# The output projection of a hybrid encoder layer as seven block products of half size, with its weight sums made during the convolution's output units

## The chip, the cores and the metric

The kernel runs on one core of one Trainium2 chip. The metric is the device time of one execution in microseconds (us), taken several times; the median counts. Beside the times there is one profiled execution, from which all durations below come. The core's engines run side by side, each with a queue of its own that it takes in order: TensorE multiplies matrices (the profile calls it PE, and PEld its weight loads), VectorE (DVE) and GpSimd (POOL) work on tiles element by element, ScalarE (ACT) applies functions and copies, SyncE (SP) issues DMAs. ScalarE issues DMAs too. They wait for one another by semaphores.

## What is computed

One layer of an encoder over 768 tokens of width 1024 (512 of a prompt, 256 of a sample, and 16 learned tokens ahead of each request). The part around the change, cut from the reference:

```python
c = jax.nn.silu(_layernorm(c, conv_ln_g[l], conv_ln_b[l]))
conv = c @ w_conv_out[l]                               # 1024 x 1024
g_a, g_c = jnp.split(jax.nn.sigmoid(gate_logits + b_gate[l]), 2, axis=-1)
h = h + (g_a * attn + g_c * conv) @ w_out[l]           # 1024 x 1024: the output projection
u = _rms(h, norm_mlp[l])
h = h + jnp.square(jax.nn.relu(u @ w_mlp_in[l])) @ w_mlp_out[l]     # the mixer, hidden 4096
```

All of it is fp32.

## The kernel before

**Products.** An fp32 product is made of three products in a rounded format (fp32r): both operands are split into a high part (rounded) and a low part (what rounding left), and high x high, high x low and low x high are added up in PSUM. So for every weight there is a supply chain. A *unit* of weights is 128 x 1024 values. SyncE loads it into one of four slots of `raw` (line 479 and, for the output projection, line 558), ScalarE rounds it into one of two `whi` (`hi_unit`, 348 to 352), GpSimd (in the stages here; elsewhere VectorE) makes the low part in one of two `wlo` (`lo_unit`, 354 to 357), TensorE multiplies. `hi_unit` of unit n waits until TensorE is through with unit n - 2, since it overwrites that one's `whi` (semaphore `unit_used`). SyncE loads a unit when the low part of the unit three before it exists.

**Stages around the change**, in TensorE's order:

1. The attention's output (`w_o_attn`), 8 units.
2. The convolution's output (`w_conv_out`, lines 2122 to 2125): 8 units, each 48 matmuls of 384 columns that fill one 128-row block m of the result. Unit m waits until block m - 2 has been read out of PSUM (`merged`).
3. The output projection (`w_out`, `token_major`, lines 2127 to 2152): tokens stand on the partitions, two halves of 512 output columns, each 4 units x 36 matmuls of 512 columns, 288 in all; 6 token tiles, one PSUM bank each. In the last unit, tile by tile, each tile's last products are followed by its addition to h on VectorE (`h_add`), its root mean square and scaling, and, ahead of the last tile, by the first transposes of the normalised rows (`first_transposes`, line 2168).
4. The mixer's first product (`w_mlp_in`), whose pairs of hidden blocks are already computed with seven half-size products instead of eight (lines 2186 to 2218; sums of weights are made by `in_sum`, and blocks of u by sums of rows), and its second product in the same manner.

**The loop over the convolution's output blocks.** For block m VectorE (1431 to 1439) multiplies the unit's result by the gate (`gconv`), adds it to the attention's part (`zacc`, semaphore `merged`), waits for ScalarE's rounding of it and makes the low part `zlo`. ScalarE (912 to 916) rounds the weights of unit m + 1 of this stage and then block m of z:

```python
for m in range(KD):
    if m > 0:
        hi_unit(act, U_CO, m // 4, m % 4 + 1)
    act.wait_ge(merged, KD + m + 1)
    nc.scalar.activation(zhi[:, m], zacc[:, m], ACT.Copy).then_inc(z_hi, 1)
```

**During the projection.** The mixer's second product needs sums of blocks of its weight. ScalarE issues their loads (`load_sums`, line 946) and stores (`store_sums`), VectorE makes them (`weight_sums`, lines 1507 to 1518, four operations of 128 x 1024 for each of two at the projection's start), ScalarE squares the rows of h (`h_square`). At the end VectorE makes four `in_sum` between the first and the last `h_add` of the second half, the reciprocals (`h_recip`), the scaling (`h_scale`, some of it on GpSimd, lines 1831 to 1836) and the low parts of the transposed rows (`u2_lo`).

## Time and profile before

| what | value |
|---|---|
| median of 3 runs | 1246.15 us (1245.69 to 1247.12) |
| the profiled execution's own time | 1246.2 us |
| its span in the trace | 1244.1 us |
| TensorE busy | 1214.2 us, 98% of the span |
| TensorE's weight loads | 1097.8 us, 88% |
| VectorE busy | 930.8 us, 75% |
| ScalarE busy | 584.7 us, 47% |
| GpSimd busy | 184.6 us, 15% |

The shares are means over stages. A stage is read by itself: how much of it TensorE is busy, at which granted clock (PEclk, 1.00 is the full 2.4 GHz), and which engine's work ends last ahead of each of TensorE's waits. In a row, `out<-in` are the names of tiles, `L948` is line 948, `x4` the number of instructions that the row holds, and what stands in brackets is the idle time of the engine ahead of the instruction, with the work whose end ended it.

### The profile page before, as it was taken

Reading aid. Unit: us, or ns where it says so; the run is one execution under the profiler, and the core shown is the slowest. Engines: PE = TensorE matmul, PEld = TensorE weight load, DVE = VectorE, ACT = ScalarE, POOL = GpSimd, SP = SyncE. Lnnn points to the kernel's source line nnn. Section 1 sums busy time; section 2 is a strip of 40 time slices with the busy share of each in tenths; the row PEclk is TensorE's granted clock in tenths of the full one; section 3 lists DMA queues with packets and bytes.
Section 4 is the critical chain, followed back from the end, with each engine's and each line's share of the span. In section 5 each row is a group of like instructions: output and inputs, shape, how many; then the busy total and the mean of one; then the engine's idle time right before and its main releaser. Section 6 shows DMA issues by size and latency. Waiting matters only on the chain.

```text
span 1244.1 us, 17971 instructions
## 1 busy us (share of the span) xinstructions
PE 1214.2 (98%) x6833; PEld 1097.8 (88%) x6833; DVE 930.8 (75%) x1192; ACT 584.7 (47%) x933; POOL 184.6 (15%) x148
## 2 busy tenths in 40 slices
PE   7999999999999999999999998899999999999997
PEld 5888888888889999989999887899999988888886
DVE  4799999998857777776653527888777767688865
ACT  6211122632246766773531136666666664444452
POOL 2000000000025444436423333000000000000001
PEclk9999999999999999999999999999999999999999
DMA  7212222334220110205335643356888459633332
GB/s 210 68 51 67 65 63 68 93 119 118 82 74 17 33 31 13 68 1 149 108 105 215 262 132 131 108 179 234 279 272 272 164 176 352 198 121 135 129 125 102
DMA packets 144370, 161.40 MB, mean 130 GB/s; under 512 B 11197, under 2 KB 111611, under 8 KB 142122
## 3 DMA queue, kind: packets, MB, share of 16 engines
q1 hardware_dynamic: 132848, 114.13, 29.5%
q10 hardware_dynamic: 11450, 46.30, 10.1%
q8 instruction: 46, 0.75, 0.2%
q14 instruction: 26, 0.21, 0.1%
HBM read 124.76 MB, written 35.65 MB: 129 GB/s over the span
## 4 chain that ended last, share of the span: by engine, by line
PE 84%; DVE 5%; ACT 4%; issue 3%; POOL 2%; ACTq 0%; POOLq 0%; DVEq 0%
PE psum L424 36%; PE psum L2236 16%; PE psum L2215 16%; PE psum L2149 4%; PE psum L2013 4%; PE psum L2045 2%; PE psum L1884 1%; POOL lnacc L1814 1%; PE psum L2025 1%; PE psum L1971 1%; DVE acc L1208 1%; PE psum L1853 1%; POOL wlo L357 1%; DVE wlo L1502 1%; ACT whi L352 0%
## 5 line engine op out<-in xcount | busy, mean ns | idle before, releaser
L2215 PE MATMUL psum<-ub,whi 128*128 128x384 f32 x896 | 229.6, 337 | 7.6 <-ACT r L942 2.3
L1208 DVE SCALAR_TENSOR_TENSOR acc<-cs,convw,acc 128x799 f32<-128x799 f32 x232 | 230.2, 1056 | 0.2
L352 ACT ACTIVATE whi<-raw 128x1024 fp32r<-128x1024 f32 (+1 forms) x80 | 79.5, 994 | 280.0 <-PE psum L424 244.5
L2215 PEld LDWEIGHTS psum<-ub,whi 128*128 128x128 f32 x896 | 162.0, 189 | 10.3 <-issue 6.5
L424 PE MATMUL psum<-uhi,wlo 128*128 128x512 f32 x592 | 152.8, 339 | 0.0
L424 PE MATMUL psum<-uhi,whi 128*128 128x512 f32 x592 | 152.2, 338 | 0.5 <-DVE wlo L357 0.5
L424 PE MATMUL psum<-ulo,whi 128*128 128x512 f32 x592 | 152.6, 339 | 0.0
L357 POOL TENSOR_TENSOR wlo<-raw,whi 128x1024 fp32r<-128x1024 f32 (+2 forms) x37 | 83.2, 2249 | 462.7 <-ACT whi L352 462.7
L2215 PE MATMUL psum<-ub,wlo 128*128 128x384 f32 x448 | 150.4, 336 | 0.0
L424 PEld LDWEIGHTS psum<-uhi,whi 128*128 128x128 f32 x592 | 91.4, 188 | 13.9 <-issue 0.8
L424 PEld LDWEIGHTS psum<-uhi,wlo 128*128 128x128 f32 x592 | 91.7, 188 | 12.9
L424 PEld LDWEIGHTS psum<-ulo,whi 128*128 128x128 f32 x592 | 91.4, 188 | 12.3
L1055 ACT ACTIVATE hidhi<-hid 128x768 fp32r<-128x768 f32 x56 | 47.4, 846 | 107.6 <-PE psum L2236 106.0
L1599 DVE TENSOR_TENSOR hidlo<-hid,hidhi 128x768 fp32r<-128x768 f32 x56 | 53.6, 957 | 44.5 <-ACT hidhi L1055 44.5
L2215 PEld LDWEIGHTS psum<-ub,wlo 128*128 128x128 f32 x448 | 84.5, 189 | 0.0
L1844 POOL TENSOR_SCALAR h<-h,rstd 128x512 f32<-128x512 f32 x3 | 3.7, 1240 | 465.0 <-DVE rstd L1675 465.0
L357 DVE TENSOR_TENSOR wlo<-raw,whi 128x1024 fp32r<-128x1024 f32 (+1 forms) x39 | 47.0, 1206 | 26.1 <-ACT whi L352 26.1
L2236 PE MATMUL psum<-whi,hidhi 128*128 128x512 f32 x168 | 65.5, 390 | 0.1
L2236 PE MATMUL psum<-wlo,hidhi 128*128 128x512 f32 x168 | 65.4, 389 | 0.0
L2236 PE MATMUL psum<-whi,hidlo 128*128 128x512 f32 x168 | 65.4, 389 | 0.0
L2236 PE MATMUL psum<-fhi,hidlo 128*128 128x512 f32 x168 | 65.4, 389 | 0.0
L2236 PE MATMUL psum<-fhi,hidhi 128*128 128x512 f32 x168 | 65.4, 389 | 0.0
(264 smaller groups left out, 2663.7 us busy)
## 6 DMA issues: line engine op xcount, KB each, us to landing
raw<-in_w_in SPq DMA_DIRECT2D x38, 512.0 KB, 3.9
wst<-in_w_mlp_out ACTq DMA_DIRECT2D x16, 1024.0 KB, 7.1
wsum<-wst ACTq DMA_DIRECT2D x16, 1024.0 KB, 5.5
raw<-in_w_mlp_in SPq DMA_DIRECT2D x32, 512.0 KB, 4.7
raw<-wsum SPq DMA_DIRECT2D x32, 512.0 KB, 3.9
raw<-in_w_mlp_out SPq DMA_DIRECT2D x24, 512.0 KB, 4.8
gates<-gout ACTq DMA_DIRECT2D x16, 384.0 KB, 2.4
gin<-gates SPq DMA_DIRECT2D x16, 384.0 KB, 3.0
```

Of the source, the lines that this page charges most:

```text
L352: nc.scalar.activation(whi[:, c % 2, 0:w], raw[:, c % 4, 0:w], ACT.Copy).then_inc(hi_ready, 1)
L357: eng.tensor_tensor(out=wlo[:, c % 2, 0:w], in0=raw[:, c % 4, 0:w], in1=whi[:, c % 2, 0:w].bitcast(F32), op=ALU.subtract).then_inc(lo_read ...
L424: mm = nc.tensor.matmul(out[:, o0:o0 + n], a, b[:, k, c0:c0 + n], start=first and step == 0, stop=last and step == 2)
L1055: nc.scalar.activation(hidhi[u % 4][:, :, :], f_block(n, c), ACT.Copy).then_inc(hidhi_ready, 1)
L1208: ins = nc.vector.scalar_tensor_tensor(out=a, in0=src, scalar=w, in1=a, op0=ALU.mult, op1=ALU.add)
L1502: nc.vector.tensor_tensor(out=wl, in0=in_source(s, j), in1=wh.bitcast(F32), op=ALU.subtract).then_inc(lo_ready, 1)
L1599: nc.vector.tensor_tensor(out=hidlo[u % 4][:, :, :], in0=f_block(n, c), in1=hidhi[u % 4][:, :, :].bitcast(F32), op=ALU.subtract).then_inc( ...
L2013: mm = nc.tensor.matmul(psum[:, q % 2, e * HALF:e * HALF + n], a[:, c0:c0 + P], b[:, grp["k0"] + k0:grp["k0"] + k0 + n], start=step == 0, ...
L2045: mm = nc.tensor.matmul(bank[:, 7, 0:2 * P], a[:, vt, hh * VD:(hh + 1) * VD], r[:, blk % 2, e, :], start=e == 0 and step == 0, stop=False)
L2149: mm = nc.tensor.matmul(out, a, b[:, kk, :], start=first and step == 0, stop=last and step == 2)
L2215: mm = nc.tensor.matmul(bank[:, IN_BANK[s % 2][j], 0:TH], a[:, k], b[:, k], start=j in (0, 1, 2, 5) and k == 0 and step == 0, stop=k == 3 ...
L2236: mm = nc.tensor.matmul(bank[:, P_BANKS[n % 2][tt]], a, b[:, kk, :], start=c == 0 and kk == 0 and step == 0, stop=c == PU - 1 and kk == 1 ...
```

## The change

The output projection takes seven products of half size (half of the sum's length, half of the columns, half of the tokens) in place of eight: with A the two halves of tokens by the two halves of the sum, B the weights' quarters, four products use sums and differences of blocks of z and of w_out (`OUT_WEIGHT`: "t" marks a product on a sum of weights, "w" one on w_out itself). It now has 14 units of 18 matmuls of 512 columns, 252 in all. A product is added to one quarter of h or stands in PSUM until others are added to it there (`OUT_BANK`), and a quarter of h is filled by additions in a table's order (`OUT_ADD`, `OUT_ON`, `OUT_FREE`).

- The sums of w_out (`out_sums`, four operations of 128 x 1024 for each of two halves c) are made on VectorE in the loop over the convolution's output blocks, in the passes m = 0 and 1, between two steps of z. ScalarE issues their loads of 4 x 1 MB ahead of that loop, behind the wait for the last low part of c, and their stores to DRAM in the passes m = 1 and 2. SyncE loads them back as units.
- In that loop ScalarE rounds, for m < 4, two 384-wide pieces of z in place of one of 768: the second after VectorE has made a difference; for m >= 4 one of 768. VectorE makes differences and low parts (two or three more operations of 384 per block). Three further blocks of z, 128 x 1536 each, are rounded and made low in the projection itself (`z_block_hi`, `z_block_lo`).
- The mixer's `weight_sums` 0 and 1 no longer stand ahead of the first `h_add` but in pieces between the `h_add` of the products. Both `load_sums` are issued ahead of the rounding of the projection's unit 1.
- The first transposes stand between units 12 and 13 of the projection: the first token rows are complete after the sixth product. In `in_sum`'s place among the last `h_add`, two now follow the scaling of tile 2 and two that of tile 5. GpSimd scales tile 0 ahead of its last `lo_unit`.
- Slots, counts of semaphores and the numbers of units are shifted to fit (`raw` slots by two, since 14 units and not 8 go before the mixer; the first weight buffer `wst` to another address); two semaphores of the layer norm become one.

The core of the diff:

```diff
@@ tables
+OUT_WEIGHT = (("w", 0, 0), ("w", 1, 0), ("t", 1, 1), ("t", 0, 0), ("t", 1, 0), ("t", 0, 1), ("w", 1, 1))
+NOUT = 2 * len(OUT_WEIGHT)
+OUT_BANK = ((4, 5, 6), (7, 0, 1), (2, 3, 7), (4, 5, 6), (2, 3, 7), (4, 5, 6), (4, 5, 6))
+OUT_ADD = ((1, 0), (1, 0), (0, 1), (0, 0), (0, 0), (0, 1), (1, 1))
+OUT_ON = {1: 0, 4: 3, 5: 2}
+OUT_FREE = {3: 0, 4: 6, 5: 9, 6: 15}
@@ SyncE
+            def out_unit(u):
+                kind, g, half = OUT_WEIGHT[u // 2]
+                sp.wait_ge(lo_ready, U_OUT + u - 3)
+                if u == 4:
+                    sp.wait_ge(wst_stored[0], 32)
+                    sp.wait_ge(wst_stored[1], 32)
+                src = wo[g, :, u % 2] if kind == "w" else osum[g, u % 2]
...
@@ ScalarE, the loop over the convolution's output blocks
+            def osum_load(c):
+                for g in range(2):
+                    act.dma_start(wsto[c][g][:, :, :], wo[g, :, c]).then_inc(wst_landed[c], 16)
+
+            def osum_store(c):
+                act.wait_ge(wst_made, 4 * (c + 1))
+                for g in range(2):
+                    act.dma_start(osum[g, c], wsto[c][g][:, :, :]).then_inc(wst_stored[c], 16)
+            act.wait_ge(unit_used, U_CO)
+            act.wait_ge(c_lo, KD)
+            osum_load(0), osum_load(1)
             for m in range(KD):
                 if m > 0:
                     hi_unit(act, U_CO, m // 4, m % 4 + 1)
                 act.wait_ge(merged, KD + m + 1)
-                nc.scalar.activation(zhi[:, m], zacc[:, m], ACT.Copy).then_inc(z_hi, 1)
+                if m < 4:
+                    nc.scalar.activation(zb[0][:, 0, m], zacc[:, m, TH:TQ], ACT.Copy).then_inc(z_hi, 1)
+                    act.wait_ge(z_made, m + 1)
+                    nc.scalar.activation(zb[2][:, 0, m], zacc[:, m, TH:TQ], ACT.Copy).then_inc(z_hi, 1)
+                else:
...
+                    nc.scalar.activation(zp[:, 0, m - 4], zacc[:, m], ACT.Copy).then_inc(z_hi, 1)
+                if m in (1, 2):
+                    osum_store(m - 1)
@@ ScalarE, the projection
             act.wait_ge(unit_used, U_OUT)
-            load_sums(0)
-            act.wait_ge(z_lo, KD)
-            load_sums(1)
+            load_sums(0), load_sums(1)
             hi_unit(act, U_OUT, 0, 1)
+            act.wait_ge(z_made, 16)
+            z_block_hi(3, zacc[:, 0:4, TH:TQ])
             hi_unit(act, U_OUT, 0, 2)
+            z_block_hi(6, zacc[:, 0:4, 0:TH])
+            for u in range(3, 6):
+                hi_unit(act, U_OUT, 0, u)
...
@@ VectorE, the loop over the convolution's output blocks
+            def out_sums(c):
+                a, b = wsto[c]
+                b11, b12, b21, b22 = a[:, :, 0:HALF], a[:, :, HALF:D], b[:, :, 0:HALF], b[:, :, HALF:D]
+                dve.wait_ge(wst_landed[c], 32)
+                nc.vector.tensor_tensor(out=b22, in0=b12, in1=b22, op=ALU.add).then_inc(wst_made, 1)
...
             for m in range(KD):
...
+                dve.wait_ge(z_hi, Z_AT[m])
+                if m < 4:
+                    nc.vector.tensor_tensor(out=zb[0][:, 1, m], in0=zacc[:, m, TH:TQ], in1=zb[0][:, 0, m].bitcast(F32), op=ALU.subtract).then_inc(z_lo, 1)
+                    nc.vector.tensor_tensor(out=zacc[:, m, TH:TQ], in0=zacc[:, m, 0:TH], in1=zacc[:, m, TH:TQ], op=ALU.subtract).then_inc(z_made, 1)
+                    if m < 2:
+                        out_sums(m)
+                    dve.wait_ge(z_hi, 2 * m + 2)
+                    nc.vector.tensor_tensor(out=zb[2][:, 1, m], in0=zacc[:, m, TH:TQ], in1=zb[2][:, 0, m].bitcast(F32), op=ALU.subtract).then_inc(z_lo, 1)
...
@@ VectorE, the projection
-            weight_sums(0), weight_sums(1)
+            z_block_lo(3, zacc[:, 0:4, TH:TQ], 1)
             h_add(0)
+            z_block_lo(6, zacc[:, 0:4, 0:TH], 2)
+            weight_sums(0, (0, 1))
+            h_add(1)
+            weight_sums(0, (2, 3))
+            h_add(2)
+            weight_sums(1, (0, 1))
+            z_block_lo(5, zacc[:, 4:KD, TH:TQ], 3)
+            h_add(3)
+            weight_sums(1, (2, 3))
+            h_add(4)
...
-            in_sum(0, 2), in_sum(0, 3), in_sum(0, 4), in_sum(0, 6)
...
+            in_sum(0, 2), in_sum(0, 3)
             for k in range(4):
                 u2_lo(k)
+            h_add(6, (0,))
...
             h_recip(4), h_recip(5), h_scale(5, hn_ready)
+            in_sum(0, 4), in_sum(0, 6)
@@ TensorE, the projection
+            for p in range(len(OUT_WEIGHT)):
+                for c in range(2):
+                    u = 2 * p + c
+                    pe.wait_ge(lo_ready, U_OUT + u + 1)
+                    wh, wl = weights(u % 2, 2, HALF)
...
+                        for step, (a, b) in enumerate(((a_hi, wh), (a_hi, wl), (a_lo, wh))):
+                            mm = nc.tensor.matmul(bank[:, OUT_BANK[p][t]], a, b[:, kk, :], start=p < 3 and c == 0 and kk == 0 and step == 0,
+                                                  stop=c == 1 and kk == 1 and step == 2, skip_group_check=True)
...
+                    if u == NOUT - 2:
+                        pe.wait_ge(hn_mid, 1)
+                        pe.wait_ge(hn_ready, 2)
+                        u_transposes(0)
```

## Rows read from the trace of the kernel before

**Rows 1.** Table of stretches (from:to, length, busy us per engine, PEclk, DMA share, GB/s).

```profile
624.60:690.90 66.30, 66.30 (x384) 66.30 (x383) 25.26 (x26) 16.99 (x19) 19.22 (x8) 1.00 0.43 147
690.90:760.90 70.00, 68.92 (x314) 56.32 (x312) 32.96 (x36) 22.66 (x43) 21.37 (x10) 1.00 0.50 179
760.90:804.30 43.40, 35.77 (x193) 32.94 (x193) 39.51 (x56) 28.93 (x54) 7.87 (x6) 0.96 0.38 123
776.30:779.40 3.10, 3.04 (x10) 3.07 (x11) 2.62 (x6) 2.57 (x4) 0.00 (x0) 0.50 0.00 0
```

**Rows 2.** TensorE's groups by line, 690.9 to 761, one of three alike.

```profile
L2149 PE MATMUL psum<-whi,zhi 128*128 128x512 f32 x96 | 37.6, 391 | 0.3 <-POOL wlo L357 0.3
```

**Rows 3.** Timeline of VectorE, 628 to 642 (start us, length us, instruction, idle before).

```profile
629.12 1.56 DVE L1414 TENSOR_TENSOR clo<-cs,chi 128x768 fp32r<-128x768 f32 x1 [0.83 <-ACT chi L905]
...
632.90 0.96 DVE L1434 TENSOR_TENSOR gconv<-psum,gin 128x768 f32<-128x768 f32 x1 [2.22 <-PE psum L424]
...
641.22 0.96 DVE L1434 TENSOR_TENSOR gconv<-psum,gin 128x768 f32<-128x768 f32 x1 [4.50 <-PE psum L424]
```

**Rows 4.** Timeline of ScalarE, 634 to 636 and 772 to 778.

```profile
634.88 0.85 ACT L916 ACTIVATE zhi<-zacc 128x768 fp32r<-128x768 f32 x1 [5.79 <-DVE zacc L1437]
635.63 1.05 ACT L352 ACTIVATE whi<-raw 128x1024 fp32r<-128x1024 f32 x1
...
772.62 0.53 ACT L1016 ACTIVATE ub<-r 128x384 fp32r<-128x384 f32 x1 [3.39 <-DVE r L1545]
...
777.69 1.48 ACT L999 ACTIVATE ub<-rt 128x1536 fp32r<-128x1536 f32 x1 [0.53 <-DVE rt L1552]
```

**Rows 5.** Timeline of GpSimd, 636 to 640.

```profile
636.75 2.40 POOL L357 TENSOR_TENSOR wlo<-raw,whi 128x1024 fp32r<-128x1024 f32 x1 [6.89 <-ACT whi L352]
```

**Rows 6.** Line 948, its 1 MB loads: issue time in ns, issue to landing.

```profile
L948 ACTq DMA_DIRECT2D wst<-in_w_mlp_out x16: 374/445/854, 693.1 to 936.1; - x16
...
DMA to landing us min/median/max: 4.8/7.1/12.8
```

**Rows 7.** Timeline of VectorE, 700 to 718 and 766 to 783.

```profile
700.54 3.47 DVE L1518 TENSOR_TENSOR wst<-wst 128x1024 f32<-128x1024 f32 x1 [5.58 <-DMA wst<-in_w_mlp_out]
...
708.24 1.22 DVE L1518 TENSOR_TENSOR wst<-wst 128x1024 f32<-128x1024 f32 x1 [0.45 <-DMA wst<-in_w_mlp_out]
709.50 4.56 DVE L1518 TENSOR_TENSOR wst<-wst,wst 128x1024 f32<-128x1024 f32 x2
...
717.61 0.69 DVE L1455 TENSOR_TENSOR h<-psum,h 128x512 f32<-128x512 f32 x1 [2.29 <-PE psum L2149]
...
766.30 2.08 DVE L1502 TENSOR_TENSOR wlo<-raw,whi 128x512 fp32r<-128x512 f32 x2
...
774.77 0.54 DVE L1549 TENSOR_TENSOR ub<-r,ub 128x384 fp32r<-128x384 f32 x1
...
782.28 1.75 DVE L1506 TENSOR_TENSOR ub<-r,ub 128x1536 fp32r<-128x1536 f32 x1
```

**Rows 8.** Timeline of GpSimd, 700 to 713.

```profile
700.53 2.39 POOL L357 TENSOR_TENSOR wlo<-raw,whi 128x1024 fp32r<-128x1024 f32 x1 [0.99 <-ACT whi L352]
...
709.89 3.08 POOL L357 TENSOR_TENSOR wlo<-raw,whi 128x1024 fp32r<-128x1024 f32 x1 [6.97 <-ACT whi L352]
```

**Rows 9.** Timeline of ScalarE's DMA queue, from 693.

```profile
693.12 2.79 ACTq L948 DMA_DIRECT2D wst<-in_w_mlp_out  x4
```

**Rows 10.** Timeline of TensorE, 699.

```profile
699.60 0.50 PE L2149 MATMUL psum<-whi,zhi 128*128 128x512 f32 x1 [0.30 <-POOL wlo L357]
```

**Rows 11.** Timeline of TensorE, 755 to 777.

```profile
755.88 2.16 PE L2162 MATMUL psum<-ident,hn 128*128 128x128 f32 x18 [0.23 <-DVE hn L1468]
...
759.44 0.47 PE L2149 MATMUL psum<-whi,zhi 128*128 128x512 f32 x1
...
762.47 0.59 PE L2215 MATMUL psum<-ub,whi 128*128 128x384 f32 x2 [1.40 <-issue]
...
776.36 0.98 PE L2215 MATMUL psum<-ub,whi 128*128 128x384 f32 x2 [2.35 <-ACT r L942]
```

More of the change, by code:

```diff
@@ L384, in in_raw @@
             k0 = HALF if j == 1 else 0
[L385 removed]
+            return (raw[:, (U_IN + 2 * s + 1) % 4, HALF:D] if j == 5 else raw[:, (U_IN + 2 * s) % 4, k0:k0 + HALF])
         def in_landed(eng, s, e):
@@ L575, in _ @@
                     gate_back(g - 3)
-            row_units(wo, U_OUT, 0)(0, [3])
-            row_units(wo, U_OUT + 4, 1)(0)
+            for u in range(3, NOUT):
+                out_unit(u)
             wi = t["w_mlp_in"][0].rearrange("(k p) n -> p k n", p=P)
@@ new lines, in z_block_lo, with h_add @@
+            def z_block_lo(j, src, made):
+                dve.wait_ge(z_hi, 12 + made)
+                nc.vector.tensor_tensor(out=zb[j][:, 1], in0=src, in1=zb[j][:, 0].bitcast(F32), op=ALU.subtract).then_inc(z_lo, 1)
+            def h_add(p, ts=range(3)):
+                m, e = OUT_ADD[p]
+                for t in ts:
+                    if t < 2:
+                        dve.wait_ge(out_tile, 2 * p + t + 1)
+                    else:
+                        dve.wait_ge(unit_used, U_OUT + 2 * p + 2)
+                    i = 3 * m + t
@@ L1821, in _ @@
             lo_unit(gp, U_O, 1, 3)
-            for n in range(U_O + KD, U_IN):
+            for n in range(U_O + KD, U_IN - 1):
                 lo_unit(gp, n - n % 4, 0, n % 4)
@@ L2125, in _ @@
                      rhs_ready=(lambda k: pe.wait_ge(c_lo, k + 1)) if m == 0 else None)
-            def token_major(base, bank0, i, units, lhs, lhs_ready, tile_done, free=lambda tt: None,
-                            at_tile=lambda tt: None):
-                for c in range(4):
-                    first_unit = isinstance(i, int) and i == 0 and c == 0
-                    last_unit = isinstance(i, int) and i == units // 4 - 1 and c == 3
-                    pe.wait_ge(lo_ready, i * 4 + (base + c + 1))
-                    wh, wl = weights(c % 2, 2, HALF)
-                    lhs_ready(i, c)
-                    by_tile = first_unit or last_unit
-                    order = [(kk, tt) for tt in range(NT) for kk in range(2)] if by_tile else \
-                            [(kk, tt) for kk in range(2) for tt in range(NT)]
-                    for kk, tt in order:
-                        first, last = first_unit and kk == 0, last_unit and kk == 1
-                        if last_unit and kk == 0:
-                            at_tile(tt)
-                        if first:
-                            free(tt)
-                        out = bank[:, (bank0 + tt) % 8]
-                        a_hi, a_lo = lhs(i, c, kk, tt)
-                        for step, (a, b) in enumerate(((a_hi, wh), (a_hi, wl), (a_lo, wh))):
-                            mm = nc.tensor.matmul(out, a, b[:, kk, :], start=first and step == 0, stop=last and step == 2)
-                        if last and tt < NT - 1:
-                            mm.then_inc(tile_done, 1)
-                    mm.then_inc(unit_used, 1)
             def u_transposes(half):
                 for k in range(KD):
-                    if half == 0 and k == 5:
-                        pe.wait_ge(h_ready, NT + 4)
-                    if half == 0 and k >= 6:
-                        pe.wait_ge(u2lo_ready, k - 5)
+                    if half == 0 and k >= 5:
+                        pe.wait_ge(u2lo_ready, k - 4)
                     if half == 1 and k >= 6:
```

209 lines of the change are left out of this document (121 added, 88 removed).

## The prediction

> **What bounds the kernel now.** I read the table of stretches first. In the convolution's output units and in the output projection TensorE is busy 66.3 of 66.3 us and 68.9 of 70.0 us; in the mixer's entry, 760.9 to 804.3, only 35.8 of 43.4, with VectorE at 39.5; after it TensorE is full again [rows 1]. So up to 760.9 an instruction taken from TensorE is time gained, but only while its weights keep coming: every unit needs ScalarE to round them, GpSimd to make the low part, and only then starts. The groups by line give the size: three groups of 96 matmuls fill the projection; of the stretch of 70.0 us the 1.1 idle and some 3.6 of transposes (costed below) go off, and 65.3 stay for 288, 0.227 us each as they follow one another [rows 2]. The timelines of VectorE, ScalarE and GpSimd then show how much room that supply has.
>
> **Removed.** Seven products of 2 units x 18 matmuls are 252 instead of 288: 36 x 0.227 = **-8.2 us**, if TensorE stays full.
>
> **Added in the convolution's output units.** In before, unit 0 ends at 632.9 and unit 1 at 641.2: 8.32 us a unit [rows 3]. ScalarE rounds z at 634.88 and then the weights of unit 2 at 635.63; GpSimd makes their low part at 636.75 for 2.40 us, done at 639.15, 2.1 us before unit 2 needs it [rows 4, 5]. The change puts the sums of w_out into VectorE's queue between that low part of z and the next unit's gate, for m = 0 and 1. Behind them wait, in order, the gate and merge of the next unit, ScalarE's two roundings of z (which wait for that merge) and, because ScalarE takes its queue in order, the rounding of the weights of unit 3 (in the pass m = 2).
>
> When do the sums end? Their loads are issued when the last c low part is done, 629.12 + 1.56 = 630.7 [rows 3]; such a load lands 4.8 to 12.8, mostly 7.1 us after its issue [rows 6]: 638. VectorE itself is there at 636.5: merge end 634.85, a 384-wide rounding and two 384-wide operations of about 0.54 each [rows 3, 4, 7]. Four sums at 1.22 are 4.9 us. But one such operation beside GpSimd's low part took 3.47, and of two in a row taking 4.56 one waited in the same way, while GpSimd waited in its turn for the operation already running (3.08 for 2.39) [rows 7, 8]. GpSimd's low part for unit 2 now falls at 638.1 to 640.5 (ScalarE's second, 384-wide rounding, 0.53, stands ahead of it [rows 4]). So for a landing between 636.5 and 640.5 the sums end at 643.8 to 645.4; I take **645**. By the Trainium skill (SBUF — State Buffer, Who interferes with whom) the two engines hold one port pair as an exclusive lock if the VectorE operation has two inputs in SBUF. The additions from PSUM, 0.69 beside a running GpSimd operation, fit that [rows 7]; by a mere sharing of bandwidth the sums would end some 2 us earlier and the sum below be 4 us lower.
>
> From the end of the sums to unit 3: low part 0.4, gate 0.99, merge 0.99, rounding 0.57, low part 0.47, difference 0.56, second rounding with the issue of the stores 0.9, weights rounded 1.14, low part and start 2.45: 8.5 us, plus 0.3 for a sum of the second set that GpSimd waits for. Unit 3 starts at 653.8 instead of 649.5. The second sums start 3.9 us after the first end, 648.9, take 4.9 + 2.4 and end at 656.2; 8.5 later, at 664.7, unit 4 can start, before it was 657.9. From m = 2 no sums stand in the way and a unit's supply takes less than 8.32 again. **+6.8 us**; with a landing at once 5.6, with the latest (643.5) 10.2; without any blocking and with the earliest landing 0.9.
>
> **The projection's weights.** A unit now lasts 18 x 0.227 = 4.1 us, not 8.2. The supply from a unit's end is 0.27 + 1.13 (rounding) + 2.40 + 0.04 = 3.8: 0.3 us of room in each unit, where there were 4.3. Call the first matmul's time T (690.9 before).
> - Unit 1: ScalarE rounds its weights only after z (T + 2.2) and after issuing four loads of about 0.45: T + 4.1 [rows 6, 9]. So they are ready at T + 7.7 to 8.0, unit 0 ends at T + 4.1: a stall of 3.6 to 4.0 (before, the same chain ended at T + 8.7 and cost 0.5 [rows 10]). After a wait of 2.35 us TensorE was granted 0.50, its 1.2 GHz level, from 776.3 to 779.4, where nine 384-wide matmuls lost 1.4 us; after a wait of 1.40 it stayed at 1.00, 2.4 GHz [rows 1, 11]. So I count the slow stretch here (in unit 3 above it hides in unit 4's wait). Either by it or by the blocks' rounding (1.5 us on ScalarE, 1.75 on VectorE [rows 4, 7]) unit 2 starts at T + 13.7 rather than T + 8.7: **+5.0**, with 3.1 and 5.5 as ends.
> - Units 3 to 13: z blocks and mixer weight sums, all with both inputs in SBUF, fill 15 us of VectorE beside 14 low parts of 2.4 us. I laid them out unit by unit: four times a VectorE operation runs when GpSimd wants to start, and costs 1.0, 0.5, 0.45 and 0.5: **+2.5**, from 0 to 5. The squares, stores and root on ScalarE lie in the 3 us free per unit, at nothing; without that room each costs its 0.8. The added raw loads (6 x 512 KB, SP) run three units ahead, at nothing; so do the rotated slots.
> - First transposes: before 755.88 to 759.44, with 0.23 of waiting ahead [rows 11]. Now the sixth already waits for u2's first low part, behind the two in_sum on VectorE: 5.7 us for waits and transposes, **+1.7** (0.5 to 2.5). Unit 13 follows and covers u2's parts: TensorE's wait of 1.4 at 762.47 is gone. But to 804.3 VectorE sets the pace [rows 1]: its first low part of weights, right after the last rows' scaling, came at 766.30, 5.4 us after the projection's end, and comes at 4.7 [rows 7]; two in_sum moved behind that scaling eat the rest. **-0.9** (-2.5 to +0.5).
>
> Sum: 6.8 - 8.2 + 5.0 + 2.5 + 1.7 - 0.9 = **+6.9**. The profiled execution took 1246.2 us (span 1244.1 and 2.1 around it), equal to the median 1246.15. Forecast: **1253**.
>
> **Rivals.**
> 1. The saving comes through (the other side). If w_out's sums are over before 641.0, so that unit 3 has its weights at 649.5, and if the units of 4.1 us get theirs in time, only -8.2 and -0.9 remain: 1237. For it: the average load of VectorE, 33 of 70 us, leaves time enough [rows 1]. Against: the sums need 4.9 us after a landing that is not before 635.5. The Trainium skill (Perfetto Trace Analysis, Identifying the Most-Contended Engine) has one optimize the engine with the highest occupancy first, which would be TensorE; in the projection it is. Chance 0.11.
> 2. The convolution's units hold (no blocking, quick loads: +0.9), the projection pays: 1246.2 + 0.9 - 8.2 + 5.0 + 2.5 + 1.7 - 0.9 = 1247. Chance 0.10.
> 3. The convolution pays, the projection's supply keeps up (4.1 holds 3.8): 1246.2 + 6.8 - 8.2 + 1.7 - 0.9 = 1246. Chance 0.08.
> 4. Loads late: landing 643.5, +10.2, and the upper ends of the collisions: 1259. Chance 0.06.
> 5. The change doesn't do what it says, TensorE runs as many matmuls as before: only the delays, 1261. The code lists 252; chance 0.01.
>
> **How the numbers follow.** The forecast, both tolls, has 0.64, with its own range 1248 to 1259. Faster or slower counts from 0.2%, 2.5 us (1243.7 and 1248.6), about what a measurement of this kernel can tell from no change. Faster: rival 1, part of 3 and edges: 0.15. Same: rival 2, most of 3, the low edge of the forecast: 0.17. Slower: the rest, 0.68. The range 1242 to 1259 leaves out rival 1 and the far end of rivals 4 and 5, about 0.17.
>
> **What would show it.** Right: idle time on TensorE ahead of the fourth and fifth convolution output units, released by GpSimd's low part, about 4 us and 1 to 3 us; sums of w_out lasting from about 638 to 645 with one operation near 3.5 us; the first projection matmul near 698; a wait of 3 to 4 us ahead of its second unit; 252 matmuls there. Wrong: output units still 8.32 us apart, or projection units 4.1 us apart from the second on. A landing before 636 or sums of 1.22 us beside GpSimd would undo the first toll, a rounding of unit 1's weights before T + 2 the second.

## The result and the profile after

The changed kernel takes 1256.58 us (median of 6 runs, 1254.85 to 1257.11), the kernel before in the same runs 1245.99: 1.0081 of its time, with an interval of 1.007 to 1.0091. It is slower by some 10.6 us; the forecast was 6.9. The span of the profiled execution grew from 1244.1 to 1255.2.

In the tables and texts below three stretches are told apart: the convolution's output units, from their first matmul to the projection's first; the projection, from there to the mixer's first; and the entry, the mixer's first 260 matmuls. In before they last 66.56, 71.53 and 57.87 us. The table of stretches of the changed kernel (columns as in [rows 1]), then three short stretches in which TensorE was granted half its clock:

```profile
623.86:699.55 75.69, 69.31 (x385) 69.02 (x385) 50.11 (x52) 18.09 (x24) 21.06 (x8) 0.95 0.66 238
699.55:770.11 70.56, 63.84 (x278) 50.52 (x278) 51.54 (x52) 34.83 (x57) 40.52 (x17) 0.98 0.64 223
770.11:830.84 60.73, 52.12 (x286) 48.88 (x284) 52.98 (x76) 38.87 (x68) 7.84 (x6) 0.97 0.52 174
...
655.40:660.70 5.30, 5.30 (x17) 5.30 (x18) 4.22 (x6) 0.94 (x2) 0.00 (x0) 0.50 0.52 159
...
708.60:711.90 3.30, 3.30 (x9) 2.61 (x8) 1.23 (x2) 0.35 (x1) 2.77 (x1) 0.50 1.02 412
...
814.50:817.70 3.20, 3.20 (x12) 3.20 (x11) 3.17 (x7) 1.44 (x4) 0.00 (x0) 0.50 1.02 416
```

So +9.1, -1.0 and +2.9: 11.0 of the 11.1. What the output units lost is read from the chain that ended last, 628 to 700 (start us, length us, what):

```profile
630.68 10.21 DMA wsto<-in_w_out
...
640.91 1.23 DVE wsto L1486
...
645.58 0.55 DVE zb L1507
...
647.04 0.97 DVE zacc L1499
648.03 0.54 ACT zb L945
...
650.65 1.06 ACT whi L366
...
651.79 3.44 POOL wlo L371
...
655.37 44.36 PE psum L438 x240
```

The load of w_out for the first sums lands after 10.21 us; the sums follow, end at 645.58, and behind them stand the gate and merge of the next block, ScalarE's roundings of it, then its rounding of the weights and GpSimd's low part: unit 3 starts at 655.37, where unit 2 had ended at 648.99. In before ScalarE turned to the weights 0.8 us after the merge's end [rows 4]. TensorE's other waits (timeline of TensorE):

```profile
707.57 0.50 PE L2267 MATMUL psum<-whi,zb 128*128 128x512 f32 x1 [3.74 <-POOL wlo L371]
...
718.25 0.50 PE L2267 MATMUL psum<-whi,zp 128*128 128x512 f32 x1 [0.61 <-POOL wlo L371]
...
785.26 0.58 PE L2306 MATMUL psum<-ub,whi 128*128 128x384 f32 x2 [3.38 <-DVE ub L1639]
...
813.25 0.59 PE L2306 MATMUL psum<-ub,whi 128*128 128x384 f32 x2 [1.80 <-DVE hid L1574]
```

The projection's second unit waits 3.74 us, where before it was 0.30 [rows 10]. Of VectorE, the second set's last sum of w_out, and the mixer's weight sums of the projection as two groups by line (count, busy us and mean ns):

```profile
653.06 3.25 DVE L1491 TENSOR_TENSOR wsto<-wsto,wsto 128x1024 f32<-128x1024 f32 x1
```

```profile
L1597 DVE TENSOR_TENSOR wst<-wst,wst 128x1024 f32<-128x1024 f32 x4 | 10.8, 2712 | 0.1
...
L1597 DVE TENSOR_TENSOR wst<-wst 128x1024 f32<-128x1024 f32 x4 | 9.2, 2288 | 0.1
```

The one sum took 3.25 instead of 1.22 us while GpSimd made a low part, and the eight weight sums took 2.71 and 2.29 us in the mean; undisturbed ones take 1.22 [rows 7]. Last the place in the entry where the two late sums of weights stand (timeline of VectorE):

```profile
773.80 0.67 DVE L1561 TENSOR_TENSOR ws<-raw,ws 128x512 f32<-128x512 f32 x1
774.40 1.48 DVE L1561 TENSOR_TENSOR ws<-raw 128x512 f32<-128x512 f32 x1
775.80 2.91 DVE L1581 TENSOR_TENSOR wlo<-raw,whi 128x512 fp32r<-128x512 f32 x2
```

They take 2.0 us between the last rows' scaling and the first low part of weights, at 775.80.

### The profile page after: what moved, and what is told of

Its sections match the earlier page's. It is cut to its first block, busy times and chain, and to the rows that moved or that the text cites. A ratio compares the mean times of both kernels' runs of the same rounds, so it can differ in the third digit from the quotient of the medians.

```text
span 1255.2 us, 17998 instructions
## 1 busy us (share of the span) xinstructions
PE 1211.4 (97%) x6797; PEld 1093.5 (87%) x6797; DVE 974.1 (78%) x1232; ACT 596.3 (48%) x946; POOL 206.5 (16%) x154
## 4 chain that ended last, share of the span: by engine, by line
PE 79%; DVE 6%; ACT 5%; issue 4%; POOL 3%; DMA 1%; ACTq 1%; POOLq 0%; DVEq 0%
PE psum L438 34%; PE psum L2327 16%; PE psum L2306 16%; PE psum L2104 4%; PE psum L2267 3%; POOL wlo L371 2%; PE psum L2136 2%; PE psum L1975 1%; PE psum L2116 1%; POOL lnacc L1904 1%; PE psum L2062 1%; ACT whi L366 1%; DMA wsto<-in_w_out 1%; DVE cs L1459 1%; DVE acc L1258 1%
## 5 line engine op out<-in xcount | busy, mean ns | idle before, releaser
L366 ACT ACTIVATE whi<-raw 128x1024 fp32r<-128x1024 f32 (+1 forms) x86 | 85.9, 998 | 278.0 <-PE psum L438 244.4
L371 POOL TENSOR_TENSOR wlo<-raw,whi 128x1024 fp32r<-128x1024 f32 (+2 forms) x43 | 103.8, 2413 | 457.1 <-ACT whi L366 457.0
L1689 DVE TENSOR_TENSOR hidlo<-hid,hidhi 128x768 fp32r<-128x768 f32 x56 | 53.6, 958 | 43.5 <-ACT hidhi L1105 43.5
L1935 POOL TENSOR_SCALAR h<-h,rstd 128x512 f32<-128x512 f32 x3 | 3.7, 1242 | 468.0 <-DVE rstd L1765 468.0
L2327 PE MATMUL psum<-flo,hidhi 128*128 128x512 f32 x168 | 65.4, 389 | 0.0
```

Of the source, the lines that this page charges most:

```text
L366: nc.scalar.activation(whi[:, c % 2, 0:w], raw[:, c % 4, 0:w], ACT.Copy).then_inc(hi_ready, 1)
L371: eng.tensor_tensor(out=wlo[:, c % 2, 0:w], in0=raw[:, c % 4, 0:w], in1=whi[:, c % 2, 0:w].bitcast(F32), op=ALU.subtract).then_inc(lo_read ...
L1689: nc.vector.tensor_tensor(out=hidlo[u % 4][:, :, :], in0=f_block(n, c), in1=hidhi[u % 4][:, :, :].bitcast(F32), op=ALU.subtract).then_inc( ...
L2327: mm = nc.tensor.matmul(bank[:, P_BANKS[n % 2][tt]], a, b[:, kk, :], start=c == 0 and kk == 0 and step == 0, stop=c == PU - 1 and kk == 1 ...
```

## The experiments

Of each run the medians and the three stretches, read as above (us); the ratio is to the kernel before on the same chip, with its interval. "On" names what a run starts from. The stretches come from one execution, whose time need not be the median: in sums_later it took 1260.92 us, in both_ahead 1247.01 and in queues_in_order 1243.02, 2.6 to 3.5 above their medians. One thing varies in them that the edits do not account for: some executions have 3.2 us at half the clock at the entry's end, which cost 1.4 to 1.6 us (last section). That holds for those of the changed kernel, sums_later, sums_later_split, conv_ahead, before_ahead and queues_in_order. So a run's total can lie that much nearer to or farther from the changed kernel's than its edit makes it; the stretches tell what the edit did.

| run | on | median | ratio | output units | projection | entry |
|---|---|---|---|---|---|---|
| before | | 1245.99 | 1 | 66.56 | 71.53 | 57.87 |
| after | | 1256.58 | 1.0081 (1.007 to 1.0091) | 75.69 | 70.56 | 60.73 |
| no_sums | after | 1248.21 | 1.0012 (1.0002 to 1.0021) | 66.74 | 70.76 | 59.15 |
| sums_later | after | 1258.29 | 1.0087 (1.007 to 1.0104) | 77.98 | 71.53 | 60.78 |
| sums_later_split | after | 1253.19 | 1.0047 (1.0031 to 1.0062) | 71.67 | 70.53 | 60.78 |
| conv_ahead | after | 1253.21 | 1.0046 (1.0029 to 1.0063) | 70.62 | 71.36 | 60.71 |
| proj_ahead | after | 1253.35 | 1.0051 (1.0034 to 1.0068) | 75.23 | 68.69 | 59.16 |
| tiny_wsums | after | 1254.01 | 1.0064 (1.0048 to 1.0081) | 76.02 | 69.03 | 59.18 |
| entry_gaps | after | 1254.05 | 1.0064 (1.0047 to 1.0081) | 75.41 | 70.59 | 57.92 |
| before_ahead | before | 1245.50 | 0.9995 (0.9985 to 1.0005) | 66.57 | 70.93 | 59.46 |
| both_ahead | after | 1243.48 | 0.9978 (0.9966 to 0.999) | 66.56 | 71.20 | 59.14 |
| queues_in_order | both_ahead | 1239.93 | 0.995 (0.9936 to 0.9963) | 66.56 | 66.46 | 59.32 |
| low_on_vector | queues_in_order | 1239.09 | 0.9939 (0.9925 to 0.9952) | 66.56 | 64.20 | 57.92 |

**no_sums: is it the sums in VectorE's queue?**

```diff
-                    if m < 2:
-                        out_sums(m)
@@ osum_store
-                act.wait_ge(wst_made, 4 * (c + 1))
+                act.wait_ge(wst_landed[c], 32)
```

> The changed kernel without VectorE's eight sums of w_out: their 4 MB are loaded and stored as before, but unsummed (this part of the computation is left out), so only the work in VectorE's queue and its wait for the loads are gone. Theory (the sums stand in VectorE's queue, and ScalarE's roundings of weights wait in line behind what comes after them): the convolution's output units stand 8.32 us apart again, TensorE waits nowhere in them, and the projection starts 9.1 us earlier: 1247.5 us (1246 to 1249). Rival (the traffic of the loads, or the smaller pieces of z, make the units late): units 3 and 4 stay late, 1254 to 1257.

The output units take 66.74 us, the whole 1248.21. In the table of stretches TensorE does not wait in them:

```profile
624.88:691.62 66.74, 66.74 (x385) 66.48 (x385) 39.08 (x44) 18.11 (x24) 20.01 (x8) 1.00 0.73 270
```

The loads are still there (270 GB/s against 147 in before), and so are the smaller pieces of z. The toll of 9.1 is the sums' place on VectorE, and the wait for the landing that they bring with them; the rival falls, and the time lies in the theory's range.

**sums_later and sums_later_split: how much of it is the landing?**

```diff
-                    if m < 2:
-                        out_sums(m)
+                    if m in (1, 2):
+                        out_sums(m - 1)
@@ ScalarE
-                if m in (1, 2):
-                    osum_store(m - 1)
+                if m in (2, 3):
+                    osum_store(m - 2)
```

> The sums of w_out one pass later each, in the passes m = 1 and 2 in place of 0 and 1, their stores likewise; nothing else moved. VectorE then no longer waits for the landing, but the 4.9 us of each four sums stay where ScalarE's queue has to wait for them. Theory (of the toll of 9.1 some 4 to 5 us are the wait for the landing, the rest the work itself): unit 3 starts on time, units 4 and 5 are late by 2 to 5 us in all: 1251.5 us (1249.5 to 1253.5). Rival (only the work counts): 1255 to 1257. Rival (only the landing counts): 1247 to 1248.

It took 1258.29, outside the ranges of the theory and of both rivals. The waits ahead of units 4 and 5 were there as the theory had them, but a third came, ahead of unit 6. ScalarE's row and TensorE's (timelines):

```profile
678.29 0.85 ACT L952 ACTIVATE zp<-zacc 128x768 fp32r<-128x768 f32 x1 [9.86 <-DMA osum<-wsto]
```

```profile
682.94 0.98 PE L438 MATMUL psum<-chi,whi 128*128 128x384 f32 x2 [3.31 <-POOL wlo L371]
```

The fifth block of z is rounded into the buffer of the sums and so waits for their store, now issued one pass later: 9.86 us of ScalarE, which holds up the weights queued behind it. The next run splits that wait by buffer:

```diff
                     if m == 4:
                         act.wait_ge(wst_stored[0], 32)
-                        act.wait_ge(wst_stored[1], 32)
@@ VectorE, k = m - 4
+                    if k == 0:
+                        dve.wait_ge(wst_stored[0], 32)
+                    if k == 1:
+                        dve.wait_ge(wst_stored[1], 32)
```

> The kernel of the run sums_later, where ScalarE's wait for both stores of the sums, ahead of the fifth block of z, is split: ScalarE waits for the first store alone, VectorE for the second ahead of the sixth block. Theory (of the 11.4 us that sums_later lost in the output units, what came from the sixth on was that wait; what stays is the two sets of sums, 2.4 us each): output units 71.3 to 73.0 us in all (sums_later 78.0, changed kernel 75.7): 1252.5 us (1251 to 1254.5), so that the wait for the landing is some 3 to 4 us of the changed kernel's toll. Rival (the sums cost as much wherever they stand on VectorE): 1256 or more.

71.67 us in the output units and 1253.19 in all. Two waits stay (timeline of TensorE):

```profile
660.02 0.69 PE L438 MATMUL psum<-chi,whi 128*128 128x384 f32 x2 [2.19 <-POOL wlo L371]
...
670.79 0.58 PE L438 MATMUL psum<-chi,whi 128*128 128x384 f32 x2 [0.60 <-POOL wlo L371]
```

So of 9.1 the earlier place, where VectorE waits for the landing, is 4.0 (75.69 against 71.67), and the sums' own work 5.1. Some 1.1 of the 4.0 is half a clock: in the changed kernel unit 4's weights were ready 9.7 us after unit 3's start, but at half the clock unit 3 itself took 10.9.

**conv_ahead: the order of ScalarE's queue.**

```diff
-                if m > 0:
-                    hi_unit(act, U_CO, m // 4, m % 4 + 1)
+                if m < KD - 1:
+                    hi_unit(act, U_CO, 0, m + 2)
```

> ScalarE rounds the weights of output unit m + 2 ahead of its roundings of block m of z, not behind them; VectorE's queue is as in the changed kernel. Theory (VectorE late by its sums, and the weights late only because ScalarE takes its queue in order): the weights come in time, but the next wait is TensorE's for the PSUM bank that VectorE's merge frees: unit 3 some 1.6 us late, unit 4 some 3.3 more: 1252.5 us (1250.5 to 1254.5). Rival (only the weights were late): 1247.5. Rival (order on ScalarE doesn't matter, the merge was the bound all along): 1256 to 1257.

1253.21, and the waits are of the kind that the theory named (timeline of TensorE):

```profile
650.74 0.62 PE L438 MATMUL psum<-chi,whi 128*128 128x384 f32 x2 [1.27 <-DVE zacc L1499]
...
661.55 0.62 PE L438 MATMUL psum<-chi,whi 128*128 128x384 f32 x2 [2.21 <-DVE zacc L1499]
```

What releases them is no longer GpSimd's low part but VectorE's merge at line 1499, late behind the sums. Out of ScalarE's way the sums cost 4.1 us instead of 9.1; the theory had 4.9.

**proj_ahead: the projection's second unit.**

```diff
@@ the last pass over the convolution's blocks
+                if m == KD - 1:
+                    hi_unit(act, U_OUT, 0, 1)
@@ the projection
             load_sums(0), load_sums(1)
-            hi_unit(act, U_OUT, 0, 1)
+            hi_unit(act, U_OUT, 0, 2)
             act.wait_ge(z_made, 16)
             z_block_hi(3, zacc[:, 0:4, TH:TQ])
-            hi_unit(act, U_OUT, 0, 2)
```

> Only the projection's start: ScalarE rounds the weights of unit 1 ahead of the last block of z and of the four loads for the mixer's sums, and those of unit 2 ahead of the first block of z that it rounds in the projection. Theory (unit 1's wait of 3.7 us and the 1.4 us at the lower clock behind it come from the place in ScalarE's queue): both vanish, 1251.5 us (1250.5 to 1252.7). Rival (GpSimd's earlier low part now runs beside VectorE's last merge and differences of z, and the wait moves to units 2 to 6): 1254 to 1257.

1253.35, between the two. Units 1 and 2 follow without a wait, but unit 3 now waits 2.37 us. TensorE's row, and ScalarE's and VectorE's ahead of it (timelines):

```profile
714.71 0.79 PE L2268 MATMUL psum<-whi,zp 128*128 128x512 f32 x1 [2.37 <-POOL wlo L371]
```

```profile
708.41 2.87 ACT L959 ACTIVATE zb<-zacc 128x1536 fp32r<-128x1536 f32 x2 [3.53 <-DVE zacc L1516]
711.18 1.04 ACT L366 ACTIVATE whi<-raw 128x1024 fp32r<-128x1024 f32 x1
```

```profile
702.49 2.16 DVE L1511 TENSOR_TENSOR zp<-zacc,zp 128x768 fp32r<-128x768 f32 x1 [0.92 <-ACT zp L954]
...
705.04 2.74 DVE L1514 TENSOR_TENSOR zacc<-zacc 128x384 f32<-128x384 f32 x1
```

Two blocks of z stand on ScalarE ahead of unit 3's weights, which had been free to be rounded from 708 on. These blocks waited 3.53 us for VectorE's last difference of z, and that was late because GpSimd's low parts, now earlier (700.82 and 704.96), ran beside VectorE's last block: the two operations took 2.16 and 2.74 us, 0.96 and 0.55 in the changed kernel. "Both vanish" was wrong: 1.9 us of the projection are won, and the rest moved down to unit 3 by what the rival named; it put the price too high.

**tiny_wsums: VectorE beside GpSimd.** The eight weight sums on 2 columns:

```diff
-    nc.vector.tensor_tensor(out=out, in0=x, in1=y, op=ALU.subtract).then_inc(wst_made, 1)
+    nc.vector.tensor_tensor(out=out[:, :, 0:1] if j < 2 else out, in0=x[:, :, 0:1] if j < 2 else x, in1=y[:, :, 0:1] if j < 2 else y, op=ALU.subtract).then_inc(wst_made, 1)
```

> The mixer's weight sums 0 and 1 are made on 2 columns in place of 1024 (the rest of them is left out), at the same places and with the same waits, so eight long operations with both inputs in SBUF go from VectorE during the projection; loads and stores stay. Theory (VectorE's long operations and GpSimd's low parts hold each other up, which costs the projection's units 2 to 13 some 2.7 us over 4.08 each): some 1.0 us of it stays, from the blocks of z: 1254.9 us (1254.2 to 1255.8). Rival (a low part of 2.4 us is too long for a unit of 4.1 by itself): no change, 1256.6.

1254.01, 0.2 below the theory's range; this execution's entry lacks the stretch at half the clock. The projection takes 69.03 against 70.56 us: 1.5 us of it are the long sums beside the low parts, the 1.1 that stay are the blocks of z and the rest. The starts of units 4 to 11 stand 4.08 us apart with their low parts still made on GpSimd, so the rival falls.

**entry_gaps: the two late sums.**

```diff
+            in_sum(0, 4)
             h_add(6, (0,))
...
             h_recip(3)
+            in_sum(0, 6)
             h_add(6, (2,))
             u2_lo(6), u2_lo(7)
             h_recip(4), h_recip(5), h_scale(5, hn_ready)
-            in_sum(0, 4), in_sum(0, 6)
```

> Only the mixer's entry: the two sums of weights that stand behind the scaling of the last rows in VectorE's queue are put into its gaps ahead of that scaling, one ahead of the first addition of the last product, one ahead of its last. Theory (in the entry VectorE sets the pace, and these two operations cost 2.15 us on its way): the entry is 1.5 us shorter: 1255.1 us (1254.2 to 1256). Rival (the entry waits for ScalarE and TensorE, as before at 776): no change, 1256.6. Rival (they delay the low parts that the transposes wait for): 1257.5.

1254.05, and the entry 57.92 us. Against 59.14 to 59.18 us in four runs with the sums at the old place (no_sums, proj_ahead, tiny_wsums, both_ahead) the place costs 1.2 us. The other 1.6 of the changed kernel's entry are the half clock at its end, which this execution lacks; the total lies just below the theory's range (1254.2).

**before_ahead: the same order without the change.** The edits of conv_ahead and of proj_ahead's first line on the kernel before.

> The kernel before with the same order on ScalarE: weights of unit m + 2 ahead of block m of z, and the projection's unit 1 ahead of the loads. Theory (with units of 8.3 us the old order had cover enough): only the 0.5 us ahead of the projection's second unit go, 1245.5 us (1245 to 1246.2), no measurable change. Rival (the order is a gain by itself, without any of the change): 1244 or less.

1245.50, a ratio whose interval holds 1; the projection is 0.6 us shorter, and no more. The entry, which the edit leaves as it is, took 59.46 us in this execution and 57.87 in before: it fell to half the clock at the end (table of stretches), as the changed kernel did.

```profile
803.65:806.85 3.20, 3.20 (x12) 3.20 (x11) 3.20 (x7) 1.14 (x2) 0.00 (x0) 0.50 0.99 376
```

The order on ScalarE is worth nothing that can be measured while a unit lasts 8.3 us.

**both_ahead: both queues.** conv_ahead, the split wait, the eight sums at the ends of three passes, and, not shown in the diff, the mixer's weight sums and their stores one place later in VectorE's and ScalarE's queues:

```diff
+            SUMS_IN = {1: ((0, 0), (0, 1), (0, 2)), 2: ((0, 3), (1, 0), (1, 1)), 3: ((1, 2), (1, 3))}
@@ pass m, behind the low part of its second piece of z
+                    for c, step in SUMS_IN.get(m, ()):
+                        out_sum(c, step)
@@ ScalarE, the projection
             load_sums(0), load_sums(1)
-            hi_unit(act, U_OUT, 0, 1)
+            hi_unit(act, U_OUT, 0, 2), hi_unit(act, U_OUT, 0, 3)
             act.wait_ge(z_made, 16)
             z_block_hi(3, zacc[:, 0:4, TH:TQ])
-            hi_unit(act, U_OUT, 0, 2)
+            hi_unit(act, U_OUT, 0, 4)
             z_block_hi(6, zacc[:, 0:4, 0:TH])
```

> The seven products with both supply chains put in order: in the convolution's output units ScalarE rounds the weights of unit m + 2 ahead of block m of z, and the eight sums of w_out are spread over the ends of VectorE's passes m = 1, 2 and 3 (three, three, two), with the wait for their stores split by buffer; in the projection the weights of units 1, 2 and 3 are rounded ahead of the blocks of z, and the mixer's weight sums come behind the second additions to h. Theory (both tolls are places in a queue, and nothing else is short): output units 8.32 to 8.5 us apart (66.6 to 67.5 in all, changed kernel 75.7), no wait of more than 1 us in the projection (from its first matmul to the mixer's first 65 to 66.5, changed kernel 70.6): 1242.8 us (1241.5 to 1245), faster than before. Rival (the waits move on once more, to the bank that the merge frees, to the stores or to a later unit): 1246 or more.

Faster than before: 0.9978 (0.9966 to 0.999). The output units are back at 66.56, with all eight sums in them. The projection is not: 71.20. VectorE's row, ScalarE's and TensorE's (timelines):

```profile
679.89 0.96 DVE L1495 TENSOR_TENSOR gconv<-psum,gin 128x768 f32<-128x768 f32 x1 [4.75 <-DMA gin<-gates]
```

```profile
696.69 0.85 ACT L950 ACTIVATE zp<-zacc 128x768 fp32r<-128x768 f32 x1 [4.87 <-DVE zacc L1498]
696.70 2.76 ACTq L987 DMA_DIRECT2D wst<-in_w_mlp_out  x4
699.56 2.00 ACT L366 ACTIVATE whi<-raw 128x1024 fp32r<-128x1024 f32 x2 [2.02 <-PE psum L2270]
```

```profile
703.10 0.79 PE L2270 MATMUL psum<-whi,zp 128*128 128x512 f32 x1 [4.22 <-POOL wlo L371]
```

VectorE waited 4.75 us for a gate's block that landed late, and lost some 2 us more in each of two differences of z beside GpSimd's low parts (2.76 and 2.64 us in place of 0.55, at 684.10 and 692.16). So the last block of z reached ScalarE late (696.69), its four loads behind it, and unit 2's weights, free to be rounded from 694.6 on, behind those. The wait had moved once more, this time behind a transfer. That is read from the rows of an execution 3.5 us slower than the median, so the other executions need not have lost as much; the next run moves the transfers and the four loads together, so the share of each is not told apart.

**queues_in_order**, three moves more:

```diff
@@ ScalarE, the projection
-            load_sums(0), load_sums(1)
-            hi_unit(act, U_OUT, 0, 2), hi_unit(act, U_OUT, 0, 3)
+            hi_unit(act, U_OUT, 0, 2)
+            load_sums(0)
+            hi_unit(act, U_OUT, 0, 3)
             act.wait_ge(z_made, 16)
             z_block_hi(3, zacc[:, 0:4, TH:TQ])
+            load_sums(1)
@@ SyncE, the loads of h
-                if g == 2 * KD:
+                if g == 2 * KD + 2:
@@ and the two in_sum as in entry_gaps
```

> The kernel of the run both_ahead with three more moves: in the projection ScalarE rounds the weights of unit 2 ahead of the four loads for the mixer's sums, which are split to both sides of unit 3's rounding; SyncE issues the loads of h two units later, behind the gate's next block; and the mixer's entry has its two sums in VectorE's gaps, as in the run entry_gaps. Theory (what both_ahead lost before its third projection unit, 4.4 us and 2.6 at the lower clock behind it, came from the place of the four loads in ScalarE's queue and from VectorE's wait of 4.8 us for a gate's block that landed late among other transfers): that wait goes, from the projection's first matmul to the mixer's first 63.5 to 65.5 us in place of 71.2, the entry 1.2 us shorter: 1236 us (1234.5 to 1239). Rival (the transfers, which keep the DMA engines busy, delay another block or the weights themselves): 1240 to 1244.

1239.93, 0.995 of before, 0.9 over the theory's range and just under the rival's. In the profiled execution the projection takes 66.46, 1 us over the bound, and the entry 59.32 in place of the 57.9 expected; the granted clock stands for both. It was halved in unit 13, which took 5.7 us and not 4.2, and at 799 in the entry (below). This execution took 3.1 us more than the median, about what the two stretches cost, so they do not explain why the median missed the range. The forecast of 1236 had taken the losses of both_ahead's profiled execution off both_ahead's median, which is 3.5 us lower; that this is the reason is not shown. The first of the two in the table of stretches:

```profile
751.70:755.00 3.30, 3.30 (x11) 2.62 (x10) 1.42 (x3) 1.45 (x3) 1.79 (x1) 0.50 0.00 0
```

**low_on_vector: no low parts on GpSimd.**

```diff
@@ VectorE, the projection
+            lo(3)
             z_block_lo(3, zacc[:, 0:4, TH:TQ], 1)
             h_add(0)
+            lo(4)
             h_add(1)
+            lo(5)
             z_block_lo(6, zacc[:, 0:4, 0:TH], 2)
-            weight_sums(0, (0, 1))
+            weight_sums(0, (0,))
+            lo(6)
+            weight_sums(0, (1,))
             h_add(2)
...
+            lo(12)
@@ GpSimd
-            for n in range(U_O + KD, U_IN - 1):
+            for n in range(U_O + KD, U_OUT + 3):
```

> The kernel of the run queues_in_order with the low parts of the projection's units 3 to 12 made by VectorE, at fixed places between its additions, sums and blocks of z, in place of GpSimd, which then stands idle there. Theory (an operation of VectorE with both inputs in SBUF and a low part on GpSimd shut each other out, which costs units 4 to 11 some 1.8 us over 4.08 each): VectorE's sums take 1.22 each again, its low parts 1.2, and the units stand 4.08 us apart: from the projection's first matmul to the mixer's first 1.5 to 2 us less than 66.5, 1238.3 us (1237 to 1240). Rival (VectorE has no room for 12 us more, additions to h and low parts wait for one another): 1241 to 1245.

1239.09, in the theory's range. VectorE's groups by line in the projection, the run's table of stretches, and TensorE's row ahead of the first transposes (timeline):

```profile
L371 DVE TENSOR_TENSOR wlo<-raw,whi 128x1024 fp32r<-128x1024 f32 x10 | 12.2, 1224 | 4.3 <-ACT whi L366 4.2
...
L1602 DVE TENSOR_TENSOR wst<-wst 128x1024 f32<-128x1024 f32 x4 | 4.9, 1222 | 0.1
L1602 DVE TENSOR_TENSOR wst<-wst,wst 128x1024 f32<-128x1024 f32 x4 | 4.9, 1218 | 0.0
```

```profile
691.06:755.26 64.20, 61.30 (x277) 49.51 (x277) 55.92 (x64) 34.74 (x57) 12.17 (x7) 1.00 0.67 238
755.26:813.18 57.92, 50.38 (x286) 47.32 (x284) 51.88 (x74) 38.98 (x68) 8.20 (x6) 1.00 0.54 182
```

```profile
746.54 1.83 PE L2249 MATMUL psum<-ident,hn 128*128 128x128 f32 x15 [1.22 <-DVE hn L1552]
```

The same weight sums take 1.22 us each, where in the changed kernel they took 2.71 and 2.29. In the timeline of TensorE the starts of units 2 to 12 stand 4.08 us apart, all of them. Against queues_in_order's execution the projection is 2.3 us shorter, but not all of it is the edit's: units 2 to 11 take 40.8 and not 42.5 us, the 1.8 of the theory; unit 12 and the first transposes take 10.5 and not 9.5, since TensorE, there earlier, now waits 1.22 us for VectorE's scaling; and unit 13 takes 4.2 and not 5.7, because this execution's clock stays at 1.00. So of the 2.3 us the edit itself is worth some 0.8. The median is 0.84 us below the run before, and the two intervals overlap, so a gain in time over queues_in_order is not shown. It is the fastest kernel of the study: 0.9939 of before, 8.4 us less in its own comparison.

## Why the prediction was right, and where it was off

The forecast was slower, 1253 in 1242 to 1259; measured are 1256.6. Both tolls that it named are there, at the places it named, and runs that take them away give the time back. Term by term, for the profiled executions (us; the projection's parts from the starts of its units in the timeline of TensorE):

| term | forecast | measured |
|---|---|---|
| output units 3 and 4 late | +6.8 | +9.1 |
| 36 matmuls fewer | -8.2 | -8.2 |
| the projection's start, until its third unit | +5.0 | +5.2 (36 matmuls in 13.86, in before 8.66) |
| units 2 to 11, VectorE beside GpSimd | +2.5 | +2.5 (ten units in 43.5, not 40.8; before had 0.1) |
| first transposes | +1.7 | +0.9 |
| the entry, with the wait ahead of it | -0.9 | +1.5 (-1.4 for the wait, +2.9) |
| sum | +6.9 | +11.0 |

**Output units.** The term that was too small is this one, and its first step the landing: forecast 7.1 us after the issue, 10.21 in the chain, inside the bound of 12.8 (the last of the four loads took 14.4). The sums ended only 1.1 us later than forecast all the same (everything runs 0.5 us earlier in this execution), since by then GpSimd's low part was over and they took 4.7 us, not 7. Most of the other 1.0 is the low part of unit 3, 3.44 us and not 2.7, because it met a sum of the second set. Unit 4 came 10.9 us after unit 3, as forecast, but by luck, for another reason: its weights were ready after 9.7, but TensorE itself, at half its clock from 655.4 to 660.7, needed 10.9. The prediction had that stretch hide in unit 4's wait. So the fifth unit shows no wait, against what was named as a sign. sums_later_split and no_sums show the two parts of the toll, 4.0 and 5.1.

**The projection.** Start, collisions and matmuls came within 0.2 us of the forecast. proj_ahead, both_ahead and queues_in_order show that the first toll is the place in ScalarE's queue; tiny_wsums and low_on_vector that the second is VectorE and GpSimd in each other's way. The Trainium skill (SBUF — State Buffer, Who interferes with whom) has the port pair that the two engines share as an exclusive lock, on which one waits for the other's whole instruction; the rows agree: the sum begun at 653.06 took 3.25 us against 1.22 and ended 1.1 us after GpSimd's low part (656.31 against 655.23), nearly its whole length, and with GpSimd idle all take 1.22.

**The entry** is the step that failed. The prediction let the two sums of weights behind the last scaling eat part of a gain; they ate all of it. The first low part of weights came 5.7 us after the projection's end (775.80 against 770.11), where it had come at 5.4 before and was forecast at 4.7, and VectorE sets the pace from there: the sums' place costs 1.2 us by entry_gaps. The wait of 1.4 us ahead of the entry did go. So the term is -0.1 and not -0.9 without the clock. The other 1.6 us, which give it the wrong sign, are the half clock at 814.5, which no step had. It is not shown to be the change's: before_ahead's entry has it too, in before's own order.

**Rivals.** The saving coming through (1237) asked for sums over before 641 and units of 4.1 us that get their weights in time. In the changed kernel neither holds, and since both tolls are there, rivals 2 and 3, which leave one out, fall as well. The fourth named the late landing, 643.5, and overshot it: the load landed at 640.9. The fifth falls by the count: TensorE ran 6797 matmuls and transposes, in before 6833. low_on_vector brings unit 3's weights and those of the short units in time by another order, and stands at 1239: the condition on the weights was the right one, and the sums need not be over for it. The Trainium skill (Perfetto Trace Analysis, Identifying the Most-Contended Engine) would have TensorE, the busiest engine, taken first: its busy time fell by 2.8 us (1211.4 against 1214.2) and the kernel became slower by 10.6. What was worth following, as the same page has it under Optimization Strategy, were the gaps on it and what ended each.

## What to carry to other kernels

When a unit of the busiest engine is cut in half, its supply keeps its length: count, in the order of each queue, what stands between "this unit's buffer is free" and "its weights are ready", and put that rounding first, ahead of work that waits for anything else; here the order of the queues, with one wait split, was worth some 13 us with the same work (both_ahead), and nothing in the kernel before, whose longer units covered it (before_ahead). Work put into the gaps of an engine costs what is queued behind it, not its own length: the same eight sums cost the output units 9.1, 4.1 (conv_ahead) or nothing (both_ahead). Put it behind what others wait for, in pieces that fit the gap. After each such move read the waits again: in four runs the wait moved on, to a PSUM bank, to a store, to a later unit, to a late load.

## What the runs showed of the hardware that was not expected

**Half a clock after like waits.** TensorE falls to 1.2 GHz after some waits and not after others that look the same. At the entry's end it waits 1.40 and 1.79 us in before and stays at 1.00; in the changed kernel it waits 1.43 and 1.80 at the same places and is granted 0.50 for the 3.2 us behind. Its longest wait in the entry, 3.38 us at 785.26, is followed by no fall, the one of 2.35 in before is [rows 1, 11]. Over the thirteen kernels' executions the last wait, 1.76 to 1.80 us in all of them, is followed by a fall in six, before_ahead among them, and by none in seven. What decides it these runs do not settle. What it costs depends on who sets the pace: entry_gaps and low_on_vector have an entry of 57.92 us each, one with a half clock where VectorE sets the pace, the other with none at all; queues_in_order, with one at 772, where VectorE sets the pace, and one at 799, where TensorE is full, has 59.32. The stretches in these three (of the last the one at 799):

```profile
783.50:786.70 3.20, 2.93 (x9) 2.96 (x10) 2.72 (x7) 2.65 (x5) 0.00 (x0) 0.50 0.00 0
```

```profile
797.15:801.00 3.85, 3.85 (x22) 3.85 (x23) 3.81 (x8) 2.97 (x6) 0.00 (x0) 1.00 0.96 369
```

```profile
799.50:802.70 3.20, 3.20 (x11) 3.20 (x11) 3.20 (x7) 1.30 (x2) 0.00 (x0) 0.50 1.01 401
```

**Transfers beside transfers.** The four loads of 1 MB for the sums landed 6.9 to 14.4 us after their issue, 11.1 in the median, while loads of the same size from before's line 948 took 7.1 [rows 6]; the DMA engines were busy for 0.66 of the output units, and 0.43 in before. In both_ahead the share is 0.77, and there a gate's block of 384 KB, issued at 663.2, landed at 679.8, 16.6 us later (the median of such loads there is 3.1), and held VectorE until 679.9.
